# A hybrid attention and retention layer on one core: the first norm's weight comes as short rows and is multiplied in behind the turning

## The reference

```
h = rmsnorm(x, norm_mix_pre)            # x * rsqrt(mean(x*x) + eps) * weight
P = h @ w_in                            # 1024 -> 3584: qA kA vA qR kR vR gR
yA = block-sparse softmax attention (8 heads) with a relative bias table
yR = retention (8 heads), group norm, swish gate
x = x + rmsnorm(concat(yA, yR) @ w_out, norm_mix_post)
h = rmsnorm(x, norm_ffn_pre)
u = conv_b + causal depthwise conv of width 3 (h @ w_up);  f = gelu(u_a) * u_b
out = x + rmsnorm(f @ w_down, norm_ffn_post)
```

## Time and profile before

| | us |
|---|---|
| runs, median (lowest to highest) | 620.61 (620.42 to 621.31) |
| span of the profiled execution, first to last instruction | 619.2 |
| PE busy | 606.9 (98%) |
| PE weight load busy | 532.1 (86%) |
| DVE busy | 473.9 (77%) |
| ACT busy | 365.0 (59%) |
| POOL busy | 143.9 (23%) |

### The profile page before, as it was taken

One profiled execution on the slowest core, in us unless ns is written; L12 is line 12 of the kernel. 1 busy time (PEld: TensorE's weight loads), 2 busy tenths in 40 slices (PEclk: granted clock), 3 DMA queues, 4 the chain that ended last, 5 costly groups with the idle time before them and its releaser, 6 DMA issues.

```text
span 619.2 us, 9966 instructions
## 1 busy us (share of the span) xinstructions
PE 606.9 (98%) x3710; PEld 532.1 (86%) x3710; DVE 473.9 (77%) x678; ACT 365.0 (59%) x571; POOL 143.9 (23%) x145
## 2 busy tenths in 40 slices
PE   8999999999999999999999999999999999899996
PEld 8888778778787877889989999999999988688885
DVE  3657548656855885978975598888999898999886
ACT  5558338536743853773844566666667655766661
POOL 4313103111310302312021222222222223422213
PEclk9999999999999999999999999999999999899999
DMA  9834223322422254681477988998899879996933
GB/s 275 241 105 127 80 69 103 102 67 68 135 68 68 102 193 157 190 242 35 103 168 145 179 169 163 218 185 177 151 224 192 174 145 180 165 223 168 238 93 136
DMA packets 87785, 93.27 MB, mean 151 GB/s; under 512 B 3049, under 2 KB 72345, under 8 KB 87746
## 3 DMA queue, kind: packets, MB, share of 16 engines
q0 software_dynamic: 26352, 35.15, 33.7%
q1 hardware_dynamic: 61394, 57.59, 29.3%
HBM read 90.62 MB, written 2.12 MB: 150 GB/s over the span
## 4 chain that ended last, share of the span: by engine, by line
PE 84%; DVE 8%; POOL 2%; issue 2%; ACT 2%; DMA 1%; DVEq 0%; SPq 0%; POOLq 0%; ACTq 0%
PE bank L694 75%; PE bank L774 1%; PE bank L836 1%; DVE ws L1940 1%; PE bank L705 1%; DMA gains<-in_norm_mix_pre_dram 1%; POOL grstd L622 1%; PE bank L825 1%; DVE xs L1648 1%; PE bank L765 1%; PE bank L764 1%; POOL work L626 1%; PE bank L815 1%; PE bank L814 1%; DVE work L1818 1%
## 5 line engine op out<-in xcount | busy, mean ns | idle before, releaser
L694 PE MATMUL bank<-hT,ws 128*128 128x256 f32 (+1 forms) x1656 | 295.3, 332 | 0.7 <-DVE work L1626 0.6
L694 PEld LDWEIGHTS bank<-hT,ws 128*128 128x128 f32 x1656 | 245.8, 190 | 28.2 <-issue 2.5
L694 PE MATMUL bank<-yT,ws 128*128 128x256 f32 x864 | 106.8, 283 | 0.0
L694 PEld LDWEIGHTS bank<-yT,ws 128*128 128x128 f32 x864 | 105.2, 192 | 0.2
L694 PE MATMUL bank<-ws,yT 128*128 128x512 f32 x366 | 88.0, 396 | 2.3 <-DVE yT L1916 2.3
L694 PEld LDWEIGHTS bank<-ws,yT 128*128 128x128 f32 x366 | 68.9, 191 | 17.0 <-issue 3.1
L1367 ACT ACTIVATE ws<-raw 128x1024 fp32r<-128x1024 f32 x46 | 48.7, 1059 | 46.1 <-PE bank L694 46.1
L1824 DVE TENSOR_TENSOR ws<-raw,ws 128x1024 fp32r<-128x1024 f32 x46 | 56.1, 1220 | 15.2 <-ACT ws L1367 15.2
L1528 DVE TENSOR_TENSOR ws<-raw,ws 128x1024 fp32r<-128x1024 f32 x47 | 57.5, 1224 | 5.8 <-ACT ws L1105 5.4
L669 POOL DMA_DIRECT2D raw<-in_w_up_dram x27 | 34.7, 1284 | 108.1 <-DVE ws L1824 103.6
L1105 ACT ACTIVATE ws<-raw 128x1024 fp32r<-128x1024 f32 x48 | 50.7, 1058 | 14.8 <-PE bank L694 10.8
(11 more groups left out here) (174 smaller groups left out, 793.5 us busy)
## 6 DMA issues: line engine op xcount, KB each, us to landing
raw<-in_w_in_dram SPq DMA_DIRECT2D x28, 512.0 KB, 4.1
raw<-in_w_up_dram POOLq DMA_DIRECT2D x27, 512.0 KB, 6.5
raw<-in_w_up_dram SPq DMA_DIRECT2D x23, 512.0 KB, 5.9
raw<-in_w_out_dram SPq DMA_DIRECT2D x16, 512.0 KB, 3.3
late<-in_w_up_dram SPq DMA_DIRECT2D x12, 512.0 KB, 6.0
raw<-in_w_down_dram POOLq DMA_DIRECT2D x12, 512.0 KB, 7.0
late<-in_w_up_dram POOLq DMA_DIRECT2D x9, 512.0 KB, 6.2
raw<-in_w_down_dram SPq DMA_DIRECT2D x9, 512.0 KB, 4.5
```

Source lines behind the costliest of these rows:

```text
L694: return nc.tensor.matmul(dst, st, mv, start=start, stop=stop, skip_group_check=onto)
```

## The change

Four things are changed, all in the first 24 us.

1. The norm's weight comes as 8 rows of 128 numbers (4 KB) instead of 128 copies of 1024 numbers. After `warm(14)` PE turns the rows into a 128x8 block of PSUM, and DVE copies it to `gcols`. Then PE does `warm(10)`. The last `warm` has 6 instead of 8.
2. DVE multiplies the rows only by 1/sqrt of the mean (`first_rows`). After PE's turn it multiplies each bank by the weight's column into `hscaled` in SBUF (`first_scale`, semaphore `h_scaled`). ACT rounds from `hscaled` (`h_round`), and DVE subtracts from `hscaled` (`first_low`). Row tiles 2 and 3 share the two halves of `hrow` and `hscaled` with tiles 0 and 1.
3. The four table loads are issued by POOL, where the clearing of `klA` and `klR` stood. The clearing moves behind the second `row_rstd`.
4. PE's table work (conv transposes, bias matmuls) moves from the end of the FRONT products to behind their first `term`; it now also waits for `h_scaled` at 4, and the second bias matmul writes bank 4 instead of bank 6.

```
-            sp.dma_start(gains[:, 0, :], norm_mix_pre[0].partition_broadcast(P)).then_inc(gains_loaded, 16)
+            sp.dma_start(grows, norm_mix_pre[0].rearrange("(k p) -> k p", p=P)).then_inc(gains_loaded, 16)
...
-            sp.wait_ge(const_set, 2)
-            sp.dma_start(relb[0:BUCKETS, :], rel_bias).then_inc(relb_loaded, 16)
-            sp.dma_start(oneh, onehot).then_inc(oneh_loaded, 16)
-            sp.dma_start(convrows[:, 0:3, :], conv_w[0].rearrange("j (t p) -> t j p", p=P)).then_inc(taps_loaded, 16)
-            sp.dma_start(convrows[:, 3, :], conv_b[0].rearrange("(t p) -> t p", p=P)).then_inc(cbias_loaded, 16)
...
             pool.wait_ge(ident_set, 2)
-            for low in (klA, klR):
-                nc.gpsimd.memset(low.bitcast(F32), 0.0).then_inc(low_cleared, 1)
+            pool.dma_start(relb[0:BUCKETS, :], rel_bias).then_inc(relb_loaded, 16)
...
             x_rstd(0)
             x_rstd(1)
+            for low in (klA, klR):
+                nc.gpsimd.memset(low.bitcast(F32), 0.0).then_inc(low_cleared, 1)
             split_lo(0)
...
-            warm(22)
+            warm(14)
+            pe.wait_ge(gains_loaded, 16)
+            nc.tensor.transpose(bank[1][:, 0:KT], grows, ident[0:KT, 0:KT]).then_inc(gcols_turned, 1)
+            warm(10)
             turn_rows(0)
             warm(2)
             turn_rows(1)
-            warm(8)
+            warm(6)
...
+            def h_round(t):
+                for half in range(2):
+                    act.wait_ge(h_scaled, 2 * t + half + 1)
+                    nc.scalar.activation(hT[:, 0, 4 * half:4 * half + 4, t * P:(t + 1) * P],
+                                         hscaled[:, t % 2, 4 * half:4 * half + 4, :], ACT.Copy).then_inc(h_hi, 1)
...
-            dve.wait_ge(gains_loaded, 16)
-            normed_rows(0)
-            normed_rows(1)
-            h_low(0)
-            h_low(1)
-            normed_rows(2)
+            def first_rows(t):
+                dve.wait_ge(rstd_done, t + 1)
+                if t >= 2:
+                    dve.wait_ge(h_turned, 2 * (t - 1))
+                nc.vector.tensor_scalar(hrow[:, t % 2, :], xs[:, t, :], rstd[:, t:t + 1], None, ALU.mult).then_inc(h_rows, 1)
+
+            def first_scale(t):
+                for half in range(2):
+                    k = slice(4 * half, 4 * half + 4)
+                    dve.wait_ge(h_turned, 2 * t + half + 1)
+                    if t >= 2:
+                        dve.wait_ge(h_hi, 2 * (t - 2) + half + 1)
+                        dve.wait_ge(h_lo, 2 * (t - 2) + half + 1)
+                    nc.vector.tensor_tensor(hscaled[:, t % 2, k, :],
+                                            bank[H_BANK[t][half]][:].rearrange("p (k c) -> p k c", k=4),
+                                            gcols[:, k].unsqueeze(2).to_broadcast([P, 4, P]), ALU.mult).then_inc(h_scaled, 1)
+
+            def first_low(t):
+                for half in range(2):
+                    k, rows = slice(4 * half, 4 * half + 4), slice(t * P, (t + 1) * P)
+                    dve.wait_ge(h_hi, 2 * t + half + 1)
+                    nc.vector.tensor_tensor(hT[:, 1, k, rows], hscaled[:, t % 2, k, :], f32(hT[:, 0, k, rows]),
+                                            ALU.subtract).then_inc(h_lo, 1)
+
+            dve.wait_ge(gcols_turned, 1)
+            nc.vector.tensor_copy(gcols[:], bank[1][:, 0:KT]).then_inc(gcols_ready, 1)
+            first_rows(0)
+            first_rows(1)
+            dve.wait_ge(gcols_ready, 1)
+            first_scale(0)
+            first_scale(1)
+            first_low(0)
+            first_low(1)
+            first_rows(2)
             split_lo(1)
-            normed_rows(3)
-            h_low(2)
-            h_low(3)
+            first_scale(2)
+            first_rows(3)
+            first_low(2)
+            first_scale(3)
+            first_low(3)
```

More of the change, by code:

```diff
@@ L232, in build @@
         gains = sb("gains", [P, 2, D])
+        gcols = sb("gcols", [P, KT])
         ident = sb("ident", [P, P])
@@ L284, in build @@
         orow = part(2048, 2048).rearrange("p (r c) -> p r c", r=2)
+        hscaled = part(2048, 2048).rearrange("p (r k c) -> p r k c", r=2, k=KT)
+        grows = work[0:KT, 5120:5120 + P]
         junk = part(4096, 1024)
@@ L577, in _ @@
             pool.wait_ge(ident_set, 2)
-            for low in (klA, klR):
-                nc.gpsimd.memset(low.bitcast(F32), 0.0).then_inc(low_cleared, 1)
+            pool.dma_start(relb[0:BUCKETS, :], rel_bias).then_inc(relb_loaded, 16)
+            pool.dma_start(oneh, onehot).then_inc(oneh_loaded, 16)
+            pool.dma_start(convrows[:, 0:3, :], conv_w[0].rearrange("j (t p) -> t j p", p=P)).then_inc(taps_loaded, 16)
+            pool.dma_start(convrows[:, 3, :], conv_b[0].rearrange("(t p) -> t p", p=P)).then_inc(cbias_loaded, 16)
             def row_rstd(t, src):
@@ L701, in turn_rows @@
                     if t == 3:
-                        pe.wait_ge(h_lo, 2)
+                        pe.wait_ge(h_scaled, 2)
                     for k in range(4):
@@ L907, in _ @@
             pe.wait_ge(const_set, 2)
-            pe.wait_ge(h_lo, 6)
-            for b, lo, hi in ((5, 0, 512), (6, 512, VEC)):
-                ins = nc.tensor.matmul(bank[b][0:HEADS, 0:hi - lo], relb[:], oneh[:, lo:hi], start=True, stop=True)
+            for b, at, lo, hi in ((5, 0, 0, 512), (4, 256, 512, VEC)):
+                ins = nc.tensor.matmul(bank[b][0:HEADS, at:at + hi - lo], relb[:], oneh[:, lo:hi], start=True, stop=True)
             ins.then_inc(bvec_made, 1)
+            pe.wait_ge(h_lo, 4)
+            term(0, 1, FRONT, False, False)
+            pe.wait_ge(w_lo_pool, 1)
+            term(0, 2, FRONT, False, True)
+            turn_rows(2)
+            pe.wait_ge(w_hi, 2)
+            pe.wait_ge(gcols_ready, 1)
+            term(1, 0, FRONT, True, False)
+            term(1, 1, FRONT, False, False)
+            turn_rows(3)
+            pe.wait_ge(w_lo, 1)
+            term(1, 2, FRONT, False, True)
             pe.wait_ge(h_hi, 2 * ST)
@@ L1134, in _ @@
             split_hi(0)
-            h_evacuate(0)
-            h_evacuate(1)
+            h_round(0)
+            h_round(1)
             x_in(2)
@@ L1139, in _ @@
             x_in(3)
-            h_evacuate(2)
-            h_evacuate(3)
+            h_round(2)
+            h_round(3)
             split_hi(2)
@@ L1149, in _ @@
             act.wait_ge(bvec_made, 1)
-            for b, lo, hi in ((5, 0, 512), (6, 512, VEC)):
-                nc.scalar.activation(bvec[:, lo:hi], bank[b][0:HEADS, 0:hi - lo], ACT.Copy, scale=8.0).then_inc(bvec_ready, 1)
+            for b, at, lo, hi in ((5, 0, 0, 512), (4, 256, 512, VEC)):
+                nc.scalar.activation(bvec[:, lo:hi], bank[b][0:HEADS, at:at + hi - lo], ACT.Copy, scale=8.0).then_inc(bvec_ready, 1)
             def stack_hi(src, keys, queries, side, signal):
```

13 lines of the change are left out of this document (2 added, 11 removed).

## The result

The kernel after takes 622.95 us (median of 11 executions, 622.17 to 625.79), the kernel before 620.55 (11 executions, 619.97 to 623.13). The ratio, paired by rounds, is 1.0049 with a 95% interval of 1.0036 to 1.0063: slower by 2 to 4 us, 0.5% of the kernel. The forecast was 620.9, within 619.7 to 622.0. The after executions come in two groups by their spans: six at 620.4 to 621.2 and five at 622.6 to 624.0. The profiled one (624.0) is of the upper group, and that has to be kept in mind with every shift read from it. Of the five, the one at 622.6 has a granted clock of 0.992 over its span; before, e2, e4 and e5 each have such executions too, 1.4 to 2.5 above their kernel's usual span, so it says nothing of the change, and four executions are left as the upper group proper.

The account below looks back on a forecast made before the run. PE, busy for 98% of the span, was taken as the bound, the end moving with the BACK products' start: 0.55 us won at the first products, 0.88 lost there, net +0.33, so 620.9 us, range 619.7 to 622.0.

Parts of the forecast that it names:

- Part 1, the start: Opening up to the first two turns: no wait for the weight, tile 0 turned at 9.14 instead of 9.79, tile 1 at 10.52.
- D: Rival: POOL's four issues and the lost port bring tile 1's rows to about 11.5, time 621.9; chance 0.05.
- S: Start of PE's first products: forecast 13.2 instead of 13.75, 0.55 us won.
- Part 2: First products, counted from tile 1's turn at 10.52: DVE's scalings and ACT's rounding let them start at 13.2.
- Part 3: Tile 2's turn to the BACK products: DVE and ACT finish tile 3 late, PE stands still for 0.88 us.
- T: PE's turn of tile 2: forecast 17.75 instead of 16.75, after 24 products and the table work.
- B: Start of the BACK products, the long run: forecast 23.47 instead of 23.14, 0.33 us later.
- Rival A: No new wait ahead of the BACK products: they start at 22.59, time 620.06; chance 0.22.
- rival B: DVE's multiplication of the rows is slow, 1.28: BACK products at 24.0, time 621.5; chance 0.1.
- rival C: The norm's weight lands late and PE's opening waits for it; landing at 8.43 gives 622.5; chance 0.1.
- Costed at nothing: POOL's four table issues, 2.5 to 5.2 us in the opening: tile 0's rows still in time, no cost.
- Nothing behind the opening changes: Nothing behind the opening hangs on a fixed time; the end moves by what the BACK products' start moves.

Follow-up runs that it names:

- e2: The changed kernel with POOL's two memsets behind its subtraction for weight unit 0 instead of ahead; 623.02 us, ratio 1.0040.
- e4: The kernel before with only the tables loaded by POOL and its clearing behind the second factor; 622.00 us, ratio 1.0021.
- e5: The kernel before with one unused tensor of 8 columns, moving every later SBUF tensor by 32 bytes; 621.73 us, ratio 1.0018.
- e11: e8 with `gcols` last in SBUF, unit 0's terms swapped and no warming between small turn and tile 0's turn; 620.18 us, ratio 0.9989.
- e3: The changed kernel with PE's table work back ahead of the BACK products; 623.21 us, ratio 1.0038.
- e6: The changed kernel with only the weight's part kept: table loads, POOL's clearing and PE's table work as before; 622.23 us, ratio 1.0025.
- e1: The changed kernel with POOL's subtraction for weight unit 0 waiting until DVE has written the rows of tiles 0 and 1; 623.07 us, ratio 1.0032.
- e7: e2 with `gcols` taken from 16 columns, moving everything behind it by 64 bytes instead of 32; 622.33 us, ratio 1.0033.
- e9: The changed kernel with `gcols` declared last in SBUF, so no other tensor moves; 622.35 us, ratio 1.0036.
- e10: The changed kernel with `gcols` last, memsets behind POOL's remainder, tables at their old place, unit 0's third term ahead of its second; 621.42 us, ratio 1.0010.
- e8: e6 with `gcols` in 16 columns, tile 0's rows multiplied ahead of the copy, and warming 12, 2, 4 around the turns; 621.14 us, ratio 1.0011.

## Why the prediction was wrong

**Part 1, the start: wrong in time.** The step "28 warming passes have begun by 6.8, the slot behind them is at 6.85" read one execution of before as fixed. PE's passes turn from slow to quick at a moment that differs by execution. PE in the windows view from 1.8 to 6.5 us (stretch, its length, busy and passes begun, granted clock, DMA share, GB/s), before and then after:

```profile
1.80:6.50 4.70, 4.65 (x26) 1.00 0.93 290
```

```profile
1.80:6.50 4.70, 4.66 (x22) 1.00 0.84 279
```

26 passes against 22, and by 7.0 it is 30 against 24. By the start times in the traces a slow pass begins 0.21 us after the last one and a quick pass 0.11. The passes turn quick at about 5.6 in before and at about 7.5 in after, and the 13 profiles are spread between 4.8 (e11) and 7.5. The granted clock reads 1.00 throughout. Before, 44 passes ended at 8.78 and PE then stood for 1.01, so a slow warming cost nothing, as e5 shows. The change took away the wait and with it the cover: tile 0 was turned at 10.42, 10.29, 10.38 and 10.09 in after, e2, e3 and e6, and at 9.17, 9.28 and 9.19 in e1, e7 and e9, with e10 between (9.56). That is up to 1.25 us between executions whose PE instructions are the same up to there, and the prediction counted a fairly quick one as certain.

**The multiply's size was right (0.75), its neighbours were not.** The prediction looked at the lost port, and priced it with "both memsets, 10.3, still ahead of 10.52". It left out the third POOL instruction, the remainder of unit 0, which follows the memsets, and it let only tile 1's multiply be caught. With the copy at 8.12 instead of 7.0, both multiplies began behind the memsets' start at 7.97: the one was held by the memsets, the other by the remainder, and tile 1's rows came at 13.1. Of the rivals it is nearest to D, which had these rows at 11.5 and a chance of 0.05. The two faults are one: without the slow warming the first multiply escapes (e1, e9), and tile 1's takes 2.3 beside the memsets alone. That was counted at nothing, being "still ahead of 10.52", and costs too: S lies 4.46 (e9) and 4.73 (e1) behind tile 0's turn, against 3.96 in e7, where POOL is quiet. PE's turn of tile 1 loses 0.1 to 0.4 of this; the rest is lost because DVE comes late to the scalings.

The clash fits the two groups of spans in after and e3, and their absence in e1, e2, e7, e10 and e11, where the remainder or both POOL instructions were kept away. That a given execution of the upper group had a slow warming was seen only in the two that were profiled (after, e3).

**Part 2: right only where DVE is free. Part 3: right.** S less tile 1's turn was to be 2.68. It is 2.64 or 2.65 in e2, e6, e7 and e10, and 3.05 or 3.06 in after, e1, e3 and e9. The sum let DVE scale tile 0 while tile 1 was being turned. When tile 1's multiply is late, tile 0's two scalings stand behind it (in after from 13.03), and tile 1's, whose first half was there at about 13.86 (13.17 + 0.69), begin only at 14.23. T to B was to be 5.72 with a wait of 0.88, and is 5.70 with 0.93 or 0.94, in after, e1, e2 and e7 alike. The cause was right as well: e3 without the table work ahead has no wait there. Rival A is refuted, rival B too (0.75 wherever POOL is quiet), rival C as well: PE never waited for the weight.

**What the tables cost: missed.** "Costed at nothing" was right for POOL's issues (four between 2.10 and 4.68, and the first factor was begun at 5.61, ahead of the 5.76 of before) and wrong for the rest. e4 has 1.3 at the median for POOL's queue in the old kernel, where unit 0's landing decides S. In the new one unit 0 has slack (landed 8.86, ACT wanted for the rows at 13.75; in e2, with the latest landing, ACT was done with it at 11.65, just ahead of the rows at 11.73), so there it costs little.

**"Nothing behind the opening changes": wrong.** Between B and M it costs 0.6 to 0.7 in all kernels with 32 bytes more in SBUF's middle (after, e1, e2, e3, e5, e6), and nothing where they are absent or last (e4, e9, e10, e11). Behind M it costs 0.3 more (e5). That is about a third of the loss, and no reading of the opening could show it.

**The sum, put right.** The opening costs 0.9 with a quick warming (e9, the same code) and 3.5 with a slow one (the profile after) instead of 0.33, and placement 1.0: 1.9 to 4.5, where the median says 2.4 and the paired ratio 3.0. Added to before's profiled span of 619.2 that is 621.1 to 623.7, close to where after's two groups lie (620.4 to 621.2 and 623.5 to 624.0). The median is an execution of the lower group. By e9 and e7 its loss in the opening is 0.4 for tile 1's multiply beside the memsets (0.91 less 0.51 at B) and 0.5 for the rest, with part 4's wait in it.

**Still open.** What lets PE's passes become quick sooner or later. It isn't the queue of the tables: with them on POOL's queue the passes turned at 5.0 (e1, e9) and at 7.5 (after), with them on SP's at 4.8 (e11) and 7.0 (e6). The end: PE's granted clock falls in some executions near 530 us (0.83 in 528 to 538 before, 0.93 after, 1.00 in e2). From M to the end of the span it takes 300.9 to 301.2 us in the six profiles where that clock is 1.00 and 301.3 to 302.1 in the seven where it fell, so the end is noisy by about a microsecond. And the ratios of e7, e8 and e9 put them 1.3 to 1.6 above what M of their profiles tells. In those profiles the passes turned quick at 5.0 to 5.7, in others as late as 7.5, which would account for 0.9 to 1.2; none of the three has a profile of a late turn to show it.

## What to carry to other kernels

Cover is part of a schedule: before taking a wait away, look which variation it hid, and count that as the new path's cost. When an instruction of POOL is moved, lay everything that POOL then has in a row, to its end, against each DVE instruction beside it, and do so for a start one microsecond late too. In a kernel like this one a new tensor in SBUF belongs behind all others, or the kernel before is timed with the same tensor unused. And before a slower row is made the cause of a shift, see whether it stands in the stretch that grew: `fx` is slower in e7 too, where the stretch from B to M is nearly whole.

## What the hardware showed that was not expected

- A shift of SBUF tensors by 32 bytes makes 672 matmuls of 128x512 float32 take 168.1 us instead of 167.4, and 36 others, on `fx`, 395 ns each instead of 389 (e5, both back in e9). With 64 bytes the first are back and the others are not (e7).
- One execution reaches quick PE passes a microsecond later than another with the same instructions (28 passes in 4.91 to 6.09 us; the change from one pass in 0.21 us to one in 0.11 comes at 4.8 to 7.5 us), at a granted clock of 1.00.
- A DVE `tensor_scalar` of 128x1024 that takes 0.75 alone takes 2.15 to 2.83 beside a POOL memset or sum; a DVE subtraction of two SBUF tensors takes 2.42 instead of 0.68 beside a POOL sum.
